# Second feed-forward matmul of a decoder block as seven block products, with the weight sums on GpSimd

## The reference

```
h = rms_norm(x, g_ffn_norm[l])                                   # x: 512 tokens x 1024
x = x + jnp.square(jax.nn.relu(h @ w_ff1[l])) @ w_ff2[l]         # w_ff1: 1024 x 4096, w_ff2: 4096 x 1024
```

## Time and profile before

| | us |
|---|---|
| median of three runs (633.29 to 633.74) | 633.36 |
| the profiled execution, its own time | 633.49 |
| span of its core in the profile | 631.8 |

### The profile page before, as it was taken

The page is one execution under the profiler, slowest core; times in us unless marked ns, Lnnn a source line. Parts: engine busy times, 40 slices in busy tenths (PEclk is TensorE's granted clock), DMA queues, the critical chain, the costliest instruction groups (busy, mean ns, idle before and its releaser), DMA issues.

```text
span 631.8 us, 8695 instructions
## 1 busy us (share of the span) xinstructions
PE 617.6 (98%) x3130; PEld 515.5 (82%) x3130; DVE 325.5 (52%) x577; ACT 264.6 (42%) x503; POOL 11.0 (2%) x31
## 2 busy tenths in 40 slices
PE   7999999999999999999999999999999999999997
PEld 5888677788898888988888888888888888888885
DVE  5699981686688686564333333334433333333323
ACT  7656552737466656462222222223333333222220
POOL 1400000000000000000000000000000000000000
PEclk9999999999999999999999999999999999999999
DMA  8512447342121020004223322332222323322003
GB/s 341 181 42 66 134 137 262 102 167 67 34 68 67 0 68 1 1 1 139 95 99 100 100 100 100 100 98 94 87 89 100 100 100 100 100 100 97 36 0 134
DMA packets 17228, 60.08 MB, mean 95 GB/s; under 512 B 2144, under 2 KB 2432, under 8 KB 17200
## 3 DMA queue, kind: packets, MB, share of 16 engines
q1 hardware_dynamic: 16416, 57.88, 27.0%
q0 software_dynamic: 640, 1.82, 0.9%
q10 hardware_dynamic: 144, 0.01, 0.0%
HBM read 57.60 MB, written 2.10 MB: 94 GB/s over the span
## 4 chain that ended last, share of the span: by engine, by line
PE 91%; DVE 4%; ACT 2%; issue 1%; POOL 0%; DVEq 0%; ACTq 0%; POOLq 0%
PE ps L317 26%; PE ps L319 25%; PE ps L318 25%; PE ps L1687 4%; PE ps L1675 2%; PE ps L1636 1%; PE ps L1422 1%; PE ps L1545 1%; PE ps L1637 1%; DVE ht_lo L955 1%; PE ps L1508 1%; PE ps L1617 1%; DVE w_lo_sb L933 1%; ACT ht_hi L564 1%; PE ps L1597 1%
## 5 line engine op out<-in xcount | busy, mean ns | idle before, releaser
L317 PE MATMUL ps<-ht_hi,w_hi_sb 128*128 128x512 f32 (+1 forms) x280 | 107.7, 385 | 0.0
L319 PE MATMUL ps<-ht_hi,w_lo_sb 128*128 128x512 f32 (+1 forms) x280 | 107.3, 383 | 0.0
L318 PE MATMUL ps<-ht_lo,w_hi_sb 128*128 128x512 f32 (+1 forms) x280 | 107.3, 383 | 0.0
L317 PE MATMUL ps<-w_hi_sb,a_hi 128*128 128x512 f32 x256 | 99.6, 389 | 0.0
L318 PE MATMUL ps<-w_lo_sb,a_hi 128*128 128x512 f32 x256 | 99.6, 389 | 0.0
L319 PE MATMUL ps<-w_hi_sb,a_lo 128*128 128x512 f32 x256 | 99.6, 389 | 0.0
L317 PE MATMUL ps<-w_hi_sb,ht_hi 128*128 128x512 f32 x192 | 82.1, 427 | 3.0 <-DVE ht_lo L955 1.6
L1293 DVE TENSOR_TENSOR w_lo_sb<-raw,w_hi_sb 128x1024 fp32r<-128x1024 f32 x64 | 78.3, 1225 | 10.2 <-ACT w_hi_sb L809 5.0
L319 PE MATMUL ps<-w_hi_sb,ht_lo 128*128 128x512 f32 x192 | 75.3, 392 | 0.0
L318 PE MATMUL ps<-w_lo_sb,ht_hi 128*128 128x512 f32 x192 | 75.1, 391 | 0.0
L1358 DVE TENSOR_TENSOR act_sb<-act_sb (+1 forms) x32 | 22.2, 692 | 102.8 <-ACT act_sb L891 102.8
(11 more groups left out here) (189 smaller groups left out, 791.0 us busy)
## 6 DMA issues: line engine op xcount, KB each, us to landing
raw<-in_w_ff SPq DMA_DIRECT2D x64, 512.0 KB, 3.4
raw<-in_w SPq DMA_DIRECT2D x24, 512.0 KB, 4.6
xs<-in_x SPq DMA_DIRECT2D x8, 512.0 KB, 6.7
raw<-in_cmp_w SPq DMA_DIRECT2D x8, 512.0 KB, 4.7
out_y<-xs SPq DMA_DIRECT2D x3, 512.0 KB, 2.7
raw<-in_w_c SPq DMA_DIRECT2D x4, 304.0 KB, 2.8
spw_sb<-in_sp_w POOLq DMA_DIRECT2D x1, 512.0 KB, 3.6
grow_ffn<-in_g_ffn POOLq DMA_DIRECT2D x1, 512.0 KB, 3.8
```

The costliest lines, as they stand in the source:

```text
L317: pe.matmul(out, l_hi, r_hi, start=start, stop=False)
L318: pe.matmul(out, l_hi, r_lo, start=False, stop=False)
L319: return pe.matmul(out, l_lo, r_hi, start=False, stop=stop)
```

## The change

The contraction of the second matmul (4096) is cut in two halves, so are its tokens (512) and its columns (1024). The eight block products are replaced by seven of a Strassen-like scheme: four of them (P1, P5, P6, P4) run as a first group over 16 steps, and three (P3, P2, P7) as a second group over 16 further steps. A step is a pair of 128-row blocks of the contraction, one from each half; each product in it is 2 groups of 128 tokens by 3 matmuls of 512 columns.

- The blocks of activations and their sums S1 to S4 lie in `aq` (six pieces of 128 x 256 per pair). VectorE forms S1, S3 and S2 in the first matmul (`sums`), and S4 in the first group (`fourth_sum`), in place of S2.
- The weight sums are made by GpSimd in place in `raw`: three subtractions of 128 x 512 per pair in the first group, one in the second.
- All weights are loaded twice over: 2 units of 128 x 1024 per step in the first group, 1.5 in the second, where a step has 24 matmuls and 18. Loads wait for `t_made` too, which counts GpSimd's subtractions.
- A step of the first group has two `w_hi`/`w_lo` of 1024 columns and one `a_hi`/`a_lo` of 1024; one of the second group has 1024 and 512 columns of weights and 768 of activations.
- Between the groups the four finished products go from PSUM into `part` (ScalarE once, VectorE three times, 128 x 1024 each), and VectorE adds them to the residual in four instructions (`base`), one in each of four steps of the second group. At the end the banks of P7, P3 and P2 are added.
- `w_ff1` and `w_ff2` are laid out in another order ahead of the launch. Some buffers move to make room.

The diff, cut to what carries this (PE's and DVE's loops before stand in lines with a minus):

```diff
+A11, S1, A22, S2, A12, A21 = range(6)
+S4, S3 = S2, A21
+FIRST = slice(A11, S2 + 1)
+SECOND = slice(S4, S3 + 1)
+PRODUCTS = {"P1": (A11, 0, 0, 0), "P5": (S1, 0, 1, 2), "P6": (S2, 1, 0, 4), "P4": (A22, 1, 1, 6),
+            "P3": (S4, 0, 0, 2), "P2": (A12, 0, 1, 0), "P7": (S3, 1, 0, 4)}
+G1, G1_LAST = ["P1", "P5", "P6", "P4"], ["P1", "P6", "P5", "P4"]
+G2, G2_FIRST = ["P3", "P2", "P7"], ["P2", "P3", "P7"]
...
+        aq = at("aq", [P, HF, 6, TH], F32, o_a)
+        part = at("part", [P, 2, 3, 512], F32, o_ht[1])
...
+            def quarters(j, J, unit, made=None):
+                sp.wait_ge(w_lo, NS + NF - RAW + 1 + 2 * J + unit)
+                if made is not None:
+                    sp.wait_ge(t_made, made)
+                sp.dma_start(raw[:, 2 * j + unit, :], w_ff2[J, unit]).then_inc(raw_in[2 * j + unit], 16)
+            def fewer(j, J, k, made):
+                sp.wait_ge(w_lo, NS + NF - RAW + 1 + 2 * J)
+                sp.wait_ge(t_made, made)
+                sp.dma_start(raw[:, 2 * j, :], w_ff2[k, 1]).then_inc(raw_in[2 * j], 16)
+                sp.wait_ge(w_lo, NS + NF - RAW + 1 + 2 * J + 1)
+                sp.dma_start(raw[:, 2 * j + 1, 0:512], w_ff2[k, 0, :, 512:]).then_inc(raw_in[2 * j + 1], 16)
+            for J in range(HF):
+                quarters(J % 2, J, 0, 3 * (J - 2) + 2 if J >= 2 else None)
+                quarters(J % 2, J, 1)
+            for k in range(HF):
+                fewer(k % 2, HF + k, k, 3 * (HF - 2 + k) + 2 if k < 2 else 3 * HF + k - 1)
...
+            b1, b2 = slice(0, 512), slice(512, 1024)
+            with pool.Fori(0, HF // 2) as i:
+                for j in range(2):
+                    a, b = 2 * j, 2 * j + 1
+                    n = i * 6 + 3 * j
+                    pool.wait_ge(raw_in[a], i * 16 + (IN + 16))
+                    pool.tensor_tensor(raw[:, a, b2], raw[:, a, b2], raw[:, a, b1], ALU.subtract).then_inc(t_made, 1)
+                    pool.wait_ge(raw_in[b], i * 16 + (IN + 16))
+                    pool.wait_ge(t_made, n + 1)
+                    pool.tensor_tensor(raw[:, b, b1], raw[:, b, b1], raw[:, a, b2], ALU.subtract).then_inc(t_made, 1)
+                    pool.wait_ge(t_made, n + 2)
+                    pool.tensor_tensor(raw[:, b, b2], raw[:, b, b1], raw[:, b, b2], ALU.subtract).then_inc(t_made, 1)
+            with pool.Fori(0, HF // 2) as i:
+                for j in range(2):
+                    a, b = 2 * j, 2 * j + 1
+                    pool.wait_ge(raw_in[a], i * 16 + (IN + 16 * (HF // 2 + 1)))
+                    pool.wait_ge(raw_in[b], i * 16 + (IN + 16 * (HF // 2 + 1)))
+                    pool.tensor_tensor(raw[:, b, b1], raw[:, a, b1], raw[:, b, b1], ALU.subtract).then_inc(t_made, 1)
...
+            def first_group(j, J):
+                form_hi(2 * j, J * 2 + (U0 - 3), J * 3 + 1)
+                form_hi(2 * j + 1, J * 2 + (U0 - 2), J * 3 + 3)
+                a_high(j, J, FIRST, J * 2 + (U0 - 2), J * 3 + 3)
...
+                def whole():
+                    form_hi(2 * j, J * 2 + (U0 - 3), loaded=i * 16 + (IN1 + 16 * (HF // 2 + 1)))
+                if not skew:
+                    whole()
+                form_hi(2 * j + 1, J * 2 + (U0 - 2), k + (3 * HF + 1), n=512)
+                a_high(j, k, SECOND, J * 2 + (U0 - 2), k + (3 * HF + 1))
...
+            act.wait_ge(p_whole, 1)
+            act.activation(part[:, :, 0, :], ps[:, 0:2, :], ACT.Copy).then_inc(p1_kept, 1)
...
+            def sums(i, j):
+                J, n = i * 2 + j // 2, i * 6 + 3 * (j // 2)
+                q = [aq[:, J, k, :] for k in range(6)]
+                dve.wait_ge(squared, i * FR + (j + 1))
+                dve.tensor_tensor(q[S1], q[A21], q[A22], ALU.add).then_inc(summed, 1)
+                dve.wait_ge(summed, n + 1)
+                dve.tensor_tensor(q[S3], q[A11], q[A21], ALU.subtract).then_inc(summed, 1)
+                dve.tensor_tensor(q[S2], q[S1], q[A11], ALU.subtract).then_inc(summed, 1)
...
+            def fourth_sum(k, count):
+                dve.wait_ge(al_done, count)
+                dve.tensor_tensor(aq[:, k, S4, :], aq[:, k, A12, :], aq[:, k, S2, :], ALU.subtract).then_inc(summed, 1)
...
-            with dve.Fori(0, NF // FR - 1) as i:
-                for j in range(FR):
-                    a_low(j % 2, i * FR + (j + 2), i * FR + (j + 3))
-                    f_lo(j, i * FR + (2 * NS + NF + FR + j + 1))
...
+            def form_lo(slot, count, n=UW):
+                dve.wait_ge(w_hi, count)
+                dve.tensor_tensor(w_lo_sb[:, FS[slot], 0:n], raw[:, slot, 0:n], w_hi_sb[:, FS[slot], 0:n].bitcast(F32),
+                                  ALU.subtract).then_inc(w_lo, 1)
+            def first_group(j, J):
+                form_lo(2 * j, J * 2 + (H0 + 1))
+                form_lo(2 * j + 1, J * 2 + (H0 + 2))
+                a_low(j, J, FIRST, J + 1)
+                fourth_sum(J, J + 1)
+            def second_group(j, i):
+                J = i * 2 + (HF + j)
+                form_lo(2 * j, J * 2 + (H0 + 1))
+                form_lo(2 * j + 1, J * 2 + (H0 + 2), 512)
+                a_low(j, i * 2 + j, SECOND, J + 1)
...
+            dve.wait_ge(p1_kept, 1)
+            dve.wait_ge(p_whole, 2)
+            dve.tensor_tensor(part[:, :, 1, :], ps[:, 4:6, :], part[:, :, 0, :], ALU.add).then_inc(kept, 1)
+            dve.wait_ge(kept, 1)
+            dve.wait_ge(w_used, U0 + 2 * HF - 1)
+            dve.tensor_tensor(part[:, :, 2, :], ps[:, 2:4, :], part[:, :, 1, :], ALU.add).then_inc(kept, 1)
+            second_group(1, 0)
+            dve.wait_ge(w_used, U0 + 2 * HF)
+            dve.tensor_tensor(part[:, :, 1, :], part[:, :, 1, :], ps[:, 6:8, :], ALU.subtract).then_inc(kept, 1)
+            def base(t):
+                rows = xs[:, t, :].rearrange("p (h n) -> p h n", h=2)
+                dve.wait_ge(r2_step, 2)
+                dve.wait_ge(kept, 3)
+                dve.scalar_tensor_tensor(out=rows, in0=part[:, t % 2, 0:3:2, :] if t < 2
+                                         else part[:, t % 2, 1:3, :], scalar=stat(rstd, "ffn", t), in1=rows,
+                                         op0=ALU.mult, op1=ALU.add).then_inc(based, 1)
+            for t in range(4):
+                second_group(t % 2, 1 + t // 2)
+                base(t)
...
-            def second(j, w_count, a_count, first=False):
-                pe.wait_ge(w_lo, w_count)
-                pe.wait_ge(al_done, a_count)
-                for t in range(NT):
-                    if first and t == NT // 2:
+            def piece(j, product, i, first, last):
+                a, unit, half, bank = PRODUCTS[product]
+                a -= (FIRST if product in G1 else SECOND).start
+                rows, c = slice(i * P, i * P + P), slice(half * 512, half * 512 + 512)
+                return three(pe, ps[:, bank + i, :], a_hi[j][:, a, rows], a_lo[j][:, a, rows],
+                             w_hi_sb[:, FS[2 * j + unit], c], w_lo_sb[:, FS[2 * j + unit], c], first, last)
+            def step(j, J, products, first=False, last=False):
+                units = [PRODUCTS[p][1] for p in products]
+                pe.wait_ge(al_done, J + 1)
+                for n, p in enumerate(products):
+                    unit = units[n]
+                    if unit not in units[:n]:
+                        pe.wait_ge(w_lo, J * 2 + (NS + NF + 1 + unit))
+                    if first and p == "P6":
                         pe.wait_ge(bank_free, NF)
-                    for b in range(2):
-                        mm = piece(j, t, slice(b * 512, b * 512 + 512), first, False)
-                mm.then_inc(w_used, 1)
...
+            def piece(j, product, i, first, last):
+                a, unit, half, bank = PRODUCTS[product]
+                a -= (FIRST if product in G1 else SECOND).start
+                rows, c = slice(i * P, i * P + P), slice(half * 512, half * 512 + 512)
+                return three(pe, ps[:, bank + i, :], a_hi[j][:, a, rows], a_lo[j][:, a, rows],
+                             w_hi_sb[:, FS[2 * j + unit], c], w_lo_sb[:, FS[2 * j + unit], c], first, last)
...
+            def step(j, J, products, first=False, last=False):
+                units = [PRODUCTS[p][1] for p in products]
+                pe.wait_ge(al_done, J + 1)
+                for n, p in enumerate(products):
+                    unit = units[n]
+                    if unit not in units[:n]:
+                        pe.wait_ge(w_lo, J * 2 + (NS + NF + 1 + unit))
+                    if first and p == "P6":
                         pe.wait_ge(bank_free, NF)
+                    if first and p == "P2":
+                        pe.wait_ge(p1_kept, 1)
+                    if first and p == "P3":
+                        pe.wait_ge(kept, 2)
+                    if first and p == "P7":
+                        pe.wait_ge(kept, 1)
+                    for i in range(2):
+                        mm = piece(j, p, i, first, last)
+                    if unit not in units[n + 1:]:
```

(83 more changed lines are left out.)

161 lines of the change are left out of this document (81 added, 80 removed).

## The result

The changed kernel takes 641.5 us (median; 640.3 to 641.7), the kernel before 633.6 beside it: a ratio of 1.012, 95% interval 1.0105 to 1.0136. 96 matmuls fewer, and slower by 8 us. The profiled execution took 641.69, its span is 639.9. Executions with a mean granted clock of 0.998 or more took 640.3 us with the changed kernel and 633.2 to 633.7 with the one before, the others (0.995 to 0.997) 641.5 to 641.7 and 634.5 to 635.1: like against like, the change costs about 7 us. The forecast was 638.0 us, slower, in a range of 620 to 652.

What follows compares the result with a forecast made beforehand. TensorE bound the kernel before; with the change, VectorE and GpSimd taking turns at SBUF would starve it. 633.5 - 21.8 + 18.9 + 7.2 + 0.2 = 638.0 us, range 620 to 652 (8 in 10).

Steps and rivals of the forecast that it cites:

- What bounds the kernel, and what is removed: Second matmul: only the number of matmuls counts; 672 in place of 768 saves 21.8 us if TensorE is fed.
- The turns: Second matmul: VectorE's two-input SBUF instructions and GpSimd's SBUF reads exclude each other; hold of 1.1 us per GpSimd subtraction.
- the one-input bound of 0.48: Lower bound of GpSimd's hold per subtraction: one input of 512 elements at 0.9 ns, nothing more for the second; 0.48 us.
- The period: Step of the first group: VectorE and GpSimd together need 6.98 us against 5.44 of TensorE, which starves.
- The first group: Its 16 steps: step 15 ends at 105.9 us where TensorE alone would need 87.0; 18.9 us lost.
- The second group: Its start: six steps at 3.98 us plus moves and `base` on VectorE, 31.9 us against TensorE's 25.8; 7.2 lost altogether.
- What costs nothing: Sums S1, S3, S2 in the first matmul and `relu` in halves hide beneath TensorE's 5.44 us per step.
- The end: After the last matmul: again two chunks of 256 columns, as now; +0.2 us at most.
- TensorE stays the bound: Rival, second matmul: GpSimd's hold is 0.48 us or the seen delay was something else; 612 us; chance 0.13 (under 620).
- The point of return: Second matmul: at a hold of 1.0 us the sum returns to 633.5; costing less than saved (620 to 632.1) had 0.17.
- The ring: Rival, second matmul: the reuse chain of `raw` becomes the bound; 652 or 645 us; chance 0.07 above 650, shared.
- The clock: Rival, second matmul: clock falls while TensorE waits; half level for a few steps, over 655 us; shares 0.07 above 650.

Runs made afterwards that it cites:

- experiment 1: Changed kernel with each GpSimd subtraction replaced by three memsets of the same 128x512 piece, so GpSimd only writes; 617.9 us (ratio 0.975).
- experiment 9: Changed kernel, GpSimd's sums kept, with the weights' hi and lo buffers 832 bytes further, 128 past a multiple of 1024; 637.3 us (1.004).
- experiment 3: Changed kernel with each GpSimd subtraction replaced by an in-place select reading one input of 128x512; 617.8 us (0.975).
- experiment 5: Kernel before, with only the buffers moved as in the changed kernel (`w_hi_sb` at byte 88384 in place of 32896); 638.5 us (1.006).
- experiment 6: Kernel before, with buffers moved as in the changed kernel but 832 bytes further (`w_hi_sb` at 89216); 634.05 us (0.9997).
- experiment 10: Changed kernel with all weight sums on VectorE, `base` in halves and `w_hi_sb` 64 bytes further, a multiple of 128; 616.7 us (0.972).
- experiment 11: Changed kernel with GpSimd's subtractions done in a tile aside that nobody waits for, one-column memsets in `raw` instead; 645.1 us (1.016).

## Why the prediction was right, point by point

- **What bounds the kernel, and what is removed.** Right: 672 matmuls in the part. That removes 21.8 us at 0.2267 each; in the changed kernel they came at 0.228 to 0.233, by the placement.
- **The turns.** Right, from one instance in the trace. The hold of a two-input subtraction was taken at 1.1 us, a delay of 1.09 was measured; the one-input bound of 0.48 stands at 0.41. Unhindered the subtraction takes 1.29 us. The rule that carried this (the Trainium skill, SBUF — State Buffer, "Who interferes with whom") also says that a GpSimd instruction which only writes does not contend with VectorE's two-input ones: experiment 1 agrees, VectorE stayed at 1.224 us. The 2.6 cycles per element that the Trainium skill gives (GPSIMD Engine Reference, "Elementwise — side-by-side cycle accounting"), 1.1 us as an estimate, agree with the 1.09.
- **The period.** 6.98 forecast, 7.03 measured. That it came out so close is luck in part, by two errors that cancelled. The forecast gave VectorE's four instructions 3.54 + 0.14 = 3.68 us and the turns 3 x 1.1 = 3.3. In the changed kernel a step of VectorE with one turn takes 559.98 - 554.88 = 5.10 us, so its own part is 5.10 - 1.09 = 4.0; the three turns add 3.0, since the one on the fourth sum costs 0.83.
- **The first group.** 18.9 us lost was forecast, 107.99 - 87.04 = 20.95 measured, of which the pace of matmuls explains little, since TensorE waits. GpSimd had finished the sums of pairs 0 to 2 at 457.97 us, at the end of the first matmul, as the forecast had it. So steps 1 to 13 run at 7.03 (the last at 6.95), and its last subtraction for the first group ended at 553.6, before step 14: steps 14 and 15 run at 5.6.
- **The second group.** 7.2 forecast, 70.09 - 65.3 = 4.8 measured (4.3 with the buffers aligned, experiment 9). Steps 18 to 21 took 5.39, 4.94, 4.88 and 4.92, the others 4.1 to 4.2. Over-sized was the term of six crowded steps at 3.98 us plus the moves: from the start of step 15 (560.3 us) to the end of `a_lo` of step 21 (589.3) VectorE took 29.0 us in place of 31.9. Its instructions start closer together than their durations, and the moves into `part` took 1.21 to 1.22 us in place of 1.28. One of the moves had GpSimd's subtraction beside it for 0.5 us, and neither was prolonged; it has one input in PSUM. Steps 16 and 17 took 4.11 and 4.20, which is the pace of the matmuls alone.
- **What costs nothing.** Here the prediction missed a term. The sums in the first matmul were free, but "buffers move to make room" stood in the description of the change and had no price in the sum. The second matmul began 4.9 us late, and the placement is 3.5 of it: 1.6 between 281 and 453 us by 1% of pace, the rest by small amounts before. In experiments 1 and 3, whose clock did not fall at the start, it began 3.5 us late with the same placement, and in experiment 9, aligned, 0.0. Experiments 5, 6, 9 and 10 show that the addresses do it. The remaining 1.4 us aren't the change's: in the profiled execution the granted clock fell back to 0.50 from 9.0 to 12.4 us. In experiment 10, with aligned buffers, it did too. The profile of the kernel before shows no such fall, though other executions of it have a mean clock of 0.997 and less. Windows of the changed kernel, the ninth run and the tenth:

```profile
9.00:12.40 3.40, 3.40 (x9) 2.62 (x9) 2.42 (x5) 2.74 (x6) 0.00 (x0) 0.50 1.02 416
```
```profile
9.00:12.40 3.40, 3.40 (x19) 2.73 (x19) 2.38 (x5) 2.95 (x7) 0.00 (x0) 1.00 1.02 417
```
```profile
8.40:11.70 3.30, 3.05 (x7) 2.47 (x8) 2.15 (x5) 3.27 (x7) 0.00 (x0) 0.50 1.02 417
```

- **The end.** +0.2 forecast; the last matmul starts 4.2 us before the end, before 4.9: -0.7.
- **The sum.** 4.9 - 21.8 + 20.95 + 4.8 - 0.7 = +8.15, measured 639.9 - 631.8 = 8.1; without the fall of the clock some 7. The forecast had +4.5 and no placement in it, so what it describes is the changed kernel aligned (experiment 9): 637.3 us beside 634.6, +2.7, and +3.0 between the two profiled executions, both without the fall. There the first group was 2.1 us dearer than forecast, the second 2.9 and the end 0.8 cheaper. The turn-taking costs only about 3 us more than is saved, so the sign was a near thing, as the prediction said. That its total of 638.0 lies only 3.5 us under the measured one owes something to luck, since a term left out and terms over-sized pull in opposite ways.
- **The rivals.** "TensorE stays the bound" at 612 us would have needed 0.48 us per turn; experiments 1 and 3 are that case, at 618. Their difference is the placement: 3.5 us ahead of the second matmul and 2.7 in it (154.99 us in place of 152.3). The point of return, 1.0 us of hold, was near, as said. The ring was no bound (1, 11). The clock did not fall over the gaps of 1.5 us in the second matmul; in experiment 11, over longer ones, it did.

## What to carry to other kernels

An idle GpSimd is no free help for a VectorE that is three quarters busy with instructions reading two tensors in SBUF: what GpSimd reads is taken out of VectorE's time (1.09 us for a two-input instruction of 512 columns that VectorE does itself in 0.61). So add up both engines' reads per step and hold the sum against the bounding engine; here the seven products pay once the sums are on VectorE (622.7 us, -1.8%), and with `base` in halves and the buffers aligned more so (616.2 us, -2.8%). And when a change moves buffers, price it: with all operands of the matmuls starting at multiples of 128 bytes the runs always had the faster pace. And compare executions of like clock before a difference of 1 or 2 us is given a cause.
